# Two transformer blocks on one core: the linear recurrence a level ahead, and two norm chains taken tile by tile

## What is computed

```python
# first block
x = x + g1 * (concat(y_fox, y_rwkv) @ w_out)
h = rms_norm(x, norm2_g) * (1 + sc2) + sh2              # the norm before the router
x = x + g2 * moe_ffn(h, ...)                            # 64 experts, 6 per token, and a shared one
x = rms_norm(x, final_g)                                # the norms between the blocks: this one
# second block
proj = rmsnorm(x, norm_mix_pre) @ w_in_2 + b_in_2       # and this one
f = lb + (1 - lb) * sigmoid(h_f); k = 1 - f; q = silu(h_q)
# linear recurrence per head: o_t = sum over s <= t of (q_t * prod of f over (s, t]) . k_s  times  v_s
o_h = hgrn2_chunkwise(q, k, log(f), h_i)
```

## Time and profile before

| | |
|---|---|
| runs of the kernel | 1540.44, 1535.65, 1539.82; median 1539.82 us |
| the profiled execution | 1537.81 us, of which its span is 1536.0 |
| mean granted TensorE clock | 0.976 |
| TensorE busy | 1430.8 us (93%) |
| VectorE busy | 683.2 us (44%) |
| ScalarE busy | 396.0 us (26%) |
| GpSimd busy | 107.2 us (7%) |
| chain that ended last | PE 61%, DVE 8%, ScalarE 1%, issue 1% |

### The profile page before, as it was taken

The page is one execution under the profiler, slowest core; times in us unless marked ns, Lnnn a source line. Parts: engine busy times, 40 slices in busy tenths (PEclk is TensorE's granted clock), DMA queues, the critical chain, the costliest instruction groups (busy, mean ns, idle before and its releaser), DMA issues.

```text
span 1536.0 us, 19978 instructions
## 1 busy us (share of the span) xinstructions
PE 1430.8 (93%) x7862; PEld 955.5 (62%) x7862; DVE 683.2 (44%) x1224; ACT 396.0 (26%) x632; POOL 107.2 (7%) x42
## 2 busy tenths in 40 slices
PE   5999998899899999999999999899997798899997
PEld 3445597888555444444444444687776457699985
DVE  3044577455662222222222223464346644667763
ACT  0121433300012222222121222145320102345443
POOL 0013336620000000000000000000000000000000
PEclk9999999999989999999999999989979999999999
DMA  8772114411744999999999997745340123155552
GB/s 315 237 254 78 65 60 165 165 56 55 281 167 179 409 420 417 413 417 419 419 404 422 415 415 289 256 145 165 87 78 7 67 76 125 56 173 185 192 192 82
DMA packets 95608, 338.83 MB, mean 221 GB/s; under 512 B 10088, under 2 KB 36361, under 8 KB 66746
## 3 DMA queue, kind: packets, MB, share of 16 engines
q1 hardware_dynamic: 84178, 319.08, 54.3%
q10 hardware_dynamic: 11113, 18.37, 4.3%
q0 software_dynamic: 256, 0.52, 0.1%
HBM read 332.94 MB, written 1.05 MB: 217 GB/s over the span
## 4 chain that ended last, share of the span: by engine, by line
PE 61%; DVE 8%; issue 1%; ACT 1%; ACTq 1%; DVEq 0%
PE bank L1732 15%; PE bank L1748 8%; PE bank L1323 6%; PE bank L1324 6%; PE bank L1325 6%; PE bank L1308 3%; PE bank L1695 3%; PE bank L1696 2%; PE bank L1713 2%; PE bank L1715 2%; PE bank L1294 1%; PE bank L1335 1%; PE bank L1704 1%; DVE xT L2182 1%; PE bank L1680 1%
## 5 line engine op out<-in xcount | busy, mean ns | idle before, releaser
L1308 PE MATMUL bank<-ring,xT 128*128 128x512 f32 (+3 forms) x480 | 191.1, 553 | 5.8 <-DVE xT L2182 3.7
L1308 PEld LDWEIGHTS bank<-ring,xT 128*128 128x128 f32 x480 | 91.1, 204 | 94.5 <-issue 85.4
L1294 PE MATMUL bank<-c_ident 128*128 128x128 f32 (+1 forms) x1042 | 134.5, 284 | 0.0
L1294 PEld LDWEIGHTS bank<-c_ident 128*128 128x128 f32 x1042 | 129.0, 200 | 5.0 <-issue 4.2
L1748 PE MATMUL bank<-dn,tmp 128*64 128x512 f32 x528 | 120.6, 598 | 0.0
L2711 DVE TENSOR_TENSOR xT<-bank,mod 128x512 fp32r<-128x512 f32 x66 | 45.7, 692 | 157.9 <-ACT mod L1051 150.7
L2704 DVE SCALAR_TENSOR_TENSOR tmp<-silu_c,rc,bank 128x256 f32<-128x256 f32 x33 | 22.6, 685 | 196.7 <-ACT silu_c L1038 191.4
L1323 PE MATMUL bank<-mod,w_high 128*128 128x256 f32 x352 | 98.6, 280 | 1.7 <-DVE xT L3142 1.7
L1324 PE MATMUL bank<-xT,w_high 128*128 128x256 f32 x352 | 98.6, 280 | 0.0
L1325 PE MATMUL bank<-mod,ring 128*128 128x256 f32 x352 | 98.2, 279 | 0.0
L3129 DVE TENSOR_TENSOR ring<-ring,w_high 128x1024 fp32r<-128x1024 f32 x66 | 77.8, 1221 | 21.9 <-ACT w_high L1243 20.2
(11 more groups left out here) (596 smaller groups left out, 2509.5 us busy)
## 6 DMA issues: line engine op xcount, KB each, us to landing
dn<-in_exp_w_down SPq DMA_DIRECT2D x66, 1024.0 KB, 10.1
ring<-in_exp_w_gate SPq DMA_DIRECT2D x34, 1024.0 KB, 9.4
ring<-in_exp_w_up SPq DMA_DIRECT2D x34, 1024.0 KB, 11.5
gu_odd<-in_exp_w_gate SPq DMA_DIRECT2D x32, 1024.0 KB, 9.8
gu_odd<-in_exp_w_up SPq DMA_DIRECT2D x32, 1024.0 KB, 11.9
ring<-in_w_ffn_in SPq DMA_DIRECT2D x22, 1024.0 KB, 5.1
ring<-in_ada_w SPq DMA_DIRECT2D x16, 1024.0 KB, 4.9
ring<-in_w_in SPq DMA_DIRECT2D x7, 2048.0 KB, 10.5
```

What stands on the lines that cost most here:

```text
L1294: pe.matmul(bank[b][:, lo:lo + width], cst["ident"][:, :], cst["ident"][:, 0:width], start=True, stop=True, skip_group_check=True)
L1308: mm = pe.matmul(bank[lin_bank(o)][:, 0:n], lhs(k, t), ring[:, j % RING, k * n:(k + 1) * n], start=(k == 0), stop=(k == kt - 1 and not bias))
```

## The change

**Out-projection and router norm.** Its four results lie in four banks, in the order tile 0 (both halves), tile 1 (both halves). VectorE does everything for tile 0, square sum and factor included, then everything for tile 1. ScalarE squares nothing. The keep-warm products change from 26 and 6 to 6 and 12.

**Between the blocks.** Also tile by tile, and both norms' squares are taken before either factor is applied: with y = x * final_g, the second norm needs the mean square of y times the first factor squared. ScalarE squares x and y of each tile; VectorE forms both factors from six small operations and one root of two columns; `xn` is y times the second factor times `norm_mix_pre`; x itself is scaled at the end. ScalarE runs one root in advance. The keep-warm products change from 50 and 4 to 32 and 8, and the small projection of tile 0 stands between the two tiles' transposes. All 25 DMAs named above are issued by GpSimd.

**Level loop.** The span sums of level l + 1 are issued before the transposes of level l, in banks 2 and 3; the exponential of l + 1 follows them, and VectorE forms the source rows of l + 1 right after it has copied the transposes of l. The source rows lie in two places in turn (`level_rows`).

```diff
@@ outputs and banks
-            if kind == "mix":
-                if jobs[j - 1][0] != "mix":
+            if kind in ("out", "mix"):
+                if jobs[j - 1][0] != kind:
...
+            first = outputs[(J_OUT, 0)]
+            if first <= o < first + 2 * T:
+                return o - first
@@ ScalarE
-            squares([x[:, 1, :]], [xn[:, 1, :]])
-            rstd(small[:, 18:20], small[:, 16:18])
+            for t in range(T):
+                rstd(small[:, 18 + t:19 + t], small[:, 16 + t:17 + t])
...
             act.sem_inc(experts_copied, 1)
-            for i, name in enumerate(GAINS):
...
+            act.activation(two_norms(0)(7), ones_pp[:, 0:1], ACT.Sqrt)
+            def square_sum(col, row, scratch):
+                asked[0] += 1
+                act.wait_ge(sq_ask, asked[0])
+                act.activation(scratch, row, ACT.Square, accum_out=col).then_inc(sq_done, 1)
+            for t in range(T):
+                c = two_norms(t)
+                square_sum(c(0), x[:, t, :], tmp[:, :])
+                square_sum(c(1), xn[:, t, :], mod[:, SC, :])
+                rstd(c(4, 2), c(2, 2))
...
+            def span_exp(level):
+                act.wait_ge(decay_mm, GH + level + 1)
+                if level >= 2:
+                    act.wait_ge(ft_src, level - 1)
+                act.activation(ex2[:, level % 2, :], bank[2 + level % 2][:, :], ACT.Exp).then_inc(hg_exp, 1)
+            span_exp(0)
+            for level in range(LEVELS + 1):
+                if level < LEVELS:
+                    span_exp(level + 1)
@@ TensorE
-                for j in range(2):
-                    for t in range(T):
-                        dense_tile(J_OUT + j, t, xTk, part=(half, 2), bank_free=(j == 1))
-            keep_warm(26, 6)
+                if half == 0:
+                    pe.wait_ge(lin_evac, outputs[(J_OUT, 0)])
+                for t in range(T):
+                    for j in range(2):
+                        dense_tile(J_OUT + j, t, xTk, part=(half, 2), bank_free=True)
+            keep_warm(6, 6)
             transpose_all(xn, layer=2, tiles=(0,))
-            keep_warm(6, 6)
+            keep_warm(12, 6)
...
-            keep_warm(50, 6)
+            keep_warm(32, 6)
             transpose_all(xn, layer=3, tiles=(0,))
-            keep_warm(4, 6)
+            pe.wait_ge(tp_evac, TP_IN2 + 2)
+            dense_tile(J_IN2, 0, xTk, bias=True)
+            keep_warm(8, 6)
             transpose_all(xn, layer=3, tiles=(1,))
             pe.wait_ge(tp_evac, TP_IN2 + 4)
-            dense(J_IN2, xTk, bias=True)
+            dense_tile(J_IN2, 1, xTk, bias=True)
...
+            def span_sums(level):
+                if level >= 2:
+                    pe.wait_ge(hg_exp, level - 1)
...
+                for t in range(T):
+                    mm = pe.matmul(bank[2 + level % 2][:, t * GW:(t + 1) * GW], spans[t], hg[:, LF, t, :],
+                                   start=True, stop=True)
+                mm.then_inc(decay_mm, 1)
             pe.wait_ge(hg_act, 3)
+            pe.wait_ge(o_used, 2)
+            span_sums(0)
             for level in range(LEVELS + 1):
+                if level < LEVELS:
+                    span_sums(level + 1)
                 keys_values_part(2 * level)
                 pe.wait_ge(ft_src, level + 1)
@@ GpSimd
+            pool.wait_ge(experts_copied, 1)
...
+            pool.wait_ge(x2_ready, 1)
+            for t in range(T):
+                pool.dma_start(mem[t], A["mem_2"][t * P:(t + 1) * P, :]).then_inc(mem_loaded, 16)
+            for i in range(len(GAINS) - N_LATE, len(GAINS)):
+                pool.dma_start(gain_of(i), bcast(A[GAINS[i]])).then_inc(late_gains, 16)
@@ VectorE, router norm
+            for t in range(T):
+                add_gated(t)
+                sum_squares(small[:, 16 + t:17 + t], x[:, t, :])
+                rsqrt_mean(small[:, 16 + t:17 + t], small[:, 16 + t:17 + t], D, RMS_EPS)
@@ VectorE, between the blocks
+            experts_gated(0)
+            add_experts(0)
+            first_scaled(0)
+            experts_gated(1)
+            dve.sem_inc(x2_ready, 1)
+            both_factors(0)
+            add_experts(1)
+            second_scaled(0)
+            first_scaled(1)
+            untranspose(tiles=(0,))
+            both_factors(1)
+            second_scaled(1)
+            untranspose(tiles=(1,))
+            for t in range(T):
+                link(dve.scalar_tensor_tensor(x[:, t, :], x[:, t, :], two_norms(t)(4), gain_of(FINAL), ...
@@ VectorE, level loop
+            level_source(0)
+            for level in range(LEVELS + 1):
+                n = SC_HG + 2 * level
                 if level:
                     dve.wait_ge(sc_mm, n)
                 pair_copy(fT)
+                if level < LEVELS:
+                    level_source(level + 1)
+                beside_level(level)
                 for parity in range(2):
```

More of the change, by code:

```diff
@@ L635, in lin_bank @@
         def lin_bank(o):
-            return o % 2 + 2 * (o in [outputs[(J_OUT + 1, t)] for t in range(T)]
-                                or o in [outputs[(("row", i), 0)] for i in range(N_ROWS)])
+            first = outputs[(J_OUT, 0)]
+            if first <= o < first + 2 * T:
+                return o - first
+            return o % 2 + 2 * (o in [outputs[(("row", i), 0)] for i in range(N_ROWS)])
         def after(j, t=0):
@@ L678, in build, with two_norms @@
         TP_FF = TP_O + 2
+        def two_norms(t):
+            return lambda i, n=1: small[:, 24 + 8 * t + i:24 + 8 * t + i + n]
         def slot(h):
@@ L1955, in _ @@
                 moba_attend(h)
-            pe.wait_ge(hg_act, 3)
-            for level in range(LEVELS + 1):
-                b = score_bank()
+            def span_sums(level):
+                if level >= 2:
+                    pe.wait_ge(hg_exp, level - 1)
                 if level < LEVELS:
@@ L2522, in _, with add_gated @@
             link(dve.scalar_tensor_tensor(mod[:, SC, :], mod[:, SC, :], 1.0, gain[:, 1, :], ALU.add, ALU.mult))
-            for j in range(2):
-                for t in range(T):
+            def add_gated(t):
+                for j in range(2):
                     o = outputs[(J_OUT + j, t)]
@@ L2547, in sums_of_squares @@
                     dve.wait_ge(sq_done, asked[0])
-            sums_of_squares(lambda t: x[:, t, :], 1)
-            rsqrt_mean(small[:, 16:18], small[:, 16:18], D, RMS_EPS)
             for t in range(T):
+                add_gated(t)
+                sum_squares(small[:, 16 + t:17 + t], x[:, t, :])
+                rsqrt_mean(small[:, 16 + t:17 + t], small[:, 16 + t:17 + t], D, RMS_EPS)
                 link(dve.scalar_tensor_tensor(tmp[:, :], x[:, t, :], small[:, 18 + t:19 + t], mod[:, SC, :],
@@ L2774, in norm_into, with experts_gated, ask_square @@
                         dve.sem_inc(ready, 1)
-            dve.wait_ge(first_gains, 32)
-            norm_into(x, x, FINAL)
-            norm_into(xn, x, MIX_PRE, ready=xn_ready)
-            untranspose()
+            def experts_gated(t):
+                for h in range(2):
+                    c = slice(h * BANK, (h + 1) * BANK)
+                    link(dve.tensor_tensor(xn[:, t, c], bank[2 * t + h][:, :], mod[:, GT, c], ALU.mult))
+            def ask_square():
+                asked[0] += 1
+                dve.sem_inc(sq_ask, 1)
@@ L3018, in _ @@
                 if level < LEVELS:
-                    link(dve.tensor_tensor(fs2, fs2, e2, ALU.mult))
+                    link(dve.tensor_tensor(rows, rows, e2, ALU.mult))
                 else:
-                    link(dve.tensor_tensor(fs2[:, 0, :], hg[:, HK, 0, :], e2[:, 0, :], ALU.mult))
-                    link(dve.tensor_tensor(fs2[:, 1, :], hg[:, HQ, 1, :], e2[:, 1, :], ALU.mult))
-                dve.sem_inc(sc_evac, 1)
+                    link(dve.tensor_tensor(rows[:, 0, :], hg[:, HK, 0, :], e2[:, 0, :], ALU.mult))
+                    link(dve.tensor_tensor(rows[:, 1, :], hg[:, HQ, 1, :], e2[:, 1, :], ALU.mult))
                 dve.sem_inc(ft_src, 1)
+            level_source(0)
+            for level in range(LEVELS + 1):
+                n = SC_HG + 2 * level
                 if level:
```

98 lines of the change are left out of this document (51 added, 47 removed).

## The result

The changed kernel takes 1516.55 us (median of 4 runs, 1515.54 to 1519.45), the kernel before beside it 1538.30 (1535.65 to 1540.44). The ratio is 0.9862, with a 95% interval of 0.9842 to 0.9882: faster by 1.4%. The profiled execution is 1515.54 with a span of 1513.6; before it was 1537.81 and 1536.0. The forecast was 1517.

A forecast was written before the change was run, and what follows sets the result against it. TensorE work was taken as the bound (61% of the span), the change priced where TensorE waits: 16.5 + 4.6 + 1.3 = 22.4 off the profiled 1537.81 gives 1515.4, or 1517 by the median; 8 in 10 is 1508 to 1526.

The forecast's parts named there:

- Level loop: Linear recurrence: cutting the chain leaves TensorE's 6.88 us per level as the period, gain 16.5, between 15 and 17.5.
- Norm between the blocks: Between experts and in-projection: tile-by-tile order and moved loads start the big products earlier, gain 4.6, bounds 1.9 and 8.4.
- the two cases: Between the blocks: big products start at 1004.0 with TensorE at full speed, 1010.5 at half speed; 1007.8 taken.
- Norm before the router: Before the router: copies start 1.9 us earlier, half speed for the second transposes costs 0.5; gain taken as 1.3.
- it was slow already, so little more can be lost there: Router: at 0.20 us an instruction, 32 in 6.41, it was taken to have little speed left to lose.
- the upper bound: Norm before the router: gain of 4, from 1.9 plus 2 of the router's 6.4 if the clock stays up.
- Rival 1: Clock up in both norm stages, argued from shorter gaps before the first transposes: gain 29, 1510.5, chance 0.13.
- Loads on GpSimd: 25 loads move to GpSimd: 21 issued by 988, landed by 1005, no stall until 1025, cost 0.
- rival 4: GpSimd's loads come late, each us past 1025 costing one; at 3 us per load 1547, chance 0.04.
- the cover of 20 us: Loads on GpSimd: the slack between landing by 1005 and the first stall at 1025.
- Rivals 3 and 5: Level loop interlocks, gain 9.4, 1524.5, chance 0.12; loop held by something else, only the norms gain, 1534, chance 0.03.
- rival 2: Clock low throughout both norm stages: 16.5 + 1.9 + 0 = 18.4, 1521.5, chance 0.13.

The follow-up runs named there:

- e9: The changed kernel with 4 more keep-warm products on TensorE in each step of the level loop: 1524.71 us, ratio 0.9916 to the kernel before.
- e10: The changed kernel without VectorE's convolution work beside levels 0 to 3, that branch's output left out: 1514.15 us, ratio 0.9848 to the kernel before.
- e3: The kernel before with only the norms between the blocks and the loads on GpSimd changed: 1536.57 us, ratio 0.9988.
- e4: The changed kernel with the 25 loads back on ScalarE: 1520.94 us, ratio 0.9893 to the kernel before.
- e2: The kernel before with only the out-projection's order and the norm before the router changed: 1539.99 us, ratio 0.9995.
- e7: The changed kernel with 28 keep-warm products instead of 12 between the two transposes ahead of the router: 1510.09 us, ratio 0.9814 to the kernel before.
- e1: The kernel before with only the level loop of the change: 1523.53 us, ratio 0.9902.
- e5: The changed kernel with GpSimd's loads held until tile 1's small in-projection is done, about 30 us later: 1526.91 us, ratio 0.9911 to the kernel before.
- e6: The changed kernel with GpSimd's loads held until the large in-projection's first block for tile 0, 46 us later: 1541.25 us, ratio 1.0007 to the kernel before.
- e12: e5 with ScalarE's root of the memory norm moved behind its first block's evacuations: 1521.47 us, ratio 0.9896 to the kernel before.

## Why the prediction was right

The time was right: 1516.55 against 1517, and 22.4 us of profiled span against a sum of 22.4. That the sum fits to a tenth is luck. The level loop gave 2.4 more than counted and the norms between the blocks 0.2 more; the router's part (1.5 less), the expert loop (0.6 longer) and the stretch behind F (0.6 longer) took it back. The sum has no term for the last two, and both go with a low clock at that place (0.50 from 978.2 to 981.6, and 0.79 behind F). What was right for its reasons is the level loop and the norms between the blocks, 21 of the 22.4.

- **Level loop, 16.5 predicted, 19.0 measured.** The mechanism was right: the chain cut, TensorE never waiting for rows of its own level, VectorE late by nothing that counts (e9, e10). The size was off by the period: 6.88 was TensorE's busy time in the window of a level, and that includes modelled ends of products which other starts overlap. The distances between starts give 6.59, 1.9 less over six full periods and the short last one. The head was 6.9 from last read to first scores, against 7.3 counted, and the tail 2.3 against 2.4.
- **Norm between the blocks, 4.6 predicted, 4.8 measured** (3.9 in e3). The steps of VectorE came as counted: tile 0's first scaled rows 9.5 us after the experts' end, 9.1 counted. The clock was between the two cases, 0.57 from 991 to 1003, over the first small projection up to the transposes of tile 1. Nearly all of the gain hangs on taking the loads off ScalarE (e4: 4.9), where the prediction had named that wait as one step among several.
- **Norm before the router, 1.3 predicted, nothing measured** (e2). The copies are 2.2 earlier, 1.9 were counted, and the clock took it all: half speed in the second transposes, in the whole router, and partly in the tables behind it. The step that failed is "it was slow already, so little more can be lost there". It also sized the other side too low: with the clock up the router takes 3.79, not 4.4, and A–B is 6.5 below the kernel before (e7), where the upper bound was 4. Rival 1 argued with the idle time before the *first* transposes, which between the blocks did shrink (from 5.40 to 1.40) without lifting the clock of C–D (0.74, before 0.80). At the router the idle time before the second transposes decided, which the new order itself had made longer (from 1.83 to 4.09). A gap of 1.83 with 6 keep-warm products doesn't keep the clock up either: with the old order the router took 6.41, 6.45 and 7.09 us (before, e1, e3).
- **Loads on GpSimd, 0 predicted, 0 measured.** They took 0.52 to 0.56 us each to issue, the first 0.76, and the 21 that VectorE asks for had landed by 997.4, so rival 4 stayed away. Its limit was wrong: not 1025 but 1018, when VectorE turns to the memory (e5, e6), since the bank evacuations of the first block stand behind its norm of the memory. Landing was assumed at 1005 and came at 997, so the cover of 20 us is what was measured, by two errors of 7 and 8 us that cancel. The rule of the Trainium skill (SBUF — State Buffer, the box on the "DVE blocks DMA" trap) did not act here: beside VectorE's two-input fp32 work the 25 issues followed each other without a gap but for one of 0.23 us, against 3.1 us each in the prediction's estimate. What late loads do cost is another thing: in e12 they helped to keep the DMA engines busy under the weight stream.
- Rivals 3 and 5 didn't happen; of rival 2 the router's half did (nothing gained), the other half not. The median stood 1.0 above the profiled execution instead of 2.0.

What stays open: F–end follows the clock behind F, but what gives one profile 1.00 there and another 0.57 isn't shown; kernels with the same code in loop and tail have all three. Each kernel has one profile, so what A–B gains by e7 is known only as 49.2 and 52.1 against 52.9 to 56.0. Whether filling the gap would have helped the old order at the router was not tried.

## What to carry to other kernels

When work is brought forward so that an engine idles in front of a thin stage, count the clock, not only the idle time: fill the gap that the new order makes, and price the thin stage at both clock levels. A load's limit is set by the first engine queue that stands behind its consumer; follow the semaphores through each in-order list (here VectorE to ScalarE's root to a bank evacuation to TensorE), not only to the data's own user. Take periods from distances between starts, not from busy sums, and judge an edit by the stretches it touches when the total varies by more than the edit is worth. A stop of TensorE costs more than its length when the work behind it runs at the low clock.

## What the runs showed of the hardware

- From A to B one and the same code took 52.9 to 56.0 us (new order, nine profiles) and 55.7 to 58.0 (old order, three), with different granted clocks; no such spread is seen in D–E (141.4 to 141.8 where no load was late). Behind F the same work took 308.8, 309.4 or 311.1 us, with a granted clock of 1.00, 0.79 or 0.57 in its first 8 us.
- The router's 32 products of 64 columns took 7.09 us at clock 0.50 in all nine profiles of the new order with 12 keep-warm products (4.1 us of idling before the transposes ahead of them in each) and 3.79 at clock 1.00 in both with 28 (0.58 us of idling).
- 25 DMAs issued by GpSimd cost 0.52 to 0.56 us each (the first 0.76) beside VectorE's fp32 products, and landed 5.1 to 14.3 us after issue.
- A weight half that ScalarE took 4.7 us after its last piece was issued in the changed kernel came 12.4 us after it in e12, with the DMA engines' busy share at 1.03 instead of 0.53.
- ScalarE took 0.32 to 0.79 us for most of its own issues in e4, and once 1.99.
